# A norm's reciprocal taken of a quarter of its elements and carried to all partitions by a store and a load

## The reference

```python
def rms_norm(x, g):
    xf = x.astype(jnp.float32)
    y = xf * lax.rsqrt(jnp.mean(xf * xf, axis=-1, keepdims=True) + RMS_EPS)
    return (y * g.astype(jnp.float32)).astype(x.dtype)

def short_conv_mixer(h, w_in, conv_w, w_out):
    bcx = h @ w_in
    b_gate, c_gate, xp = bcx[..., :D], bcx[..., D:2 * D], bcx[..., 2 * D:]
    u = c_gate * xp
    u_conv = causal_depthwise_conv3(u, conv_w)
    return (b_gate * u_conv) @ w_out

def swiglu(h, w_gate, w_up, w_down):
    return (jax.nn.silu(h @ w_gate) * (h @ w_up)) @ w_down

for i in range(2):
    h = h + mixer_i(rms_norm(h, mixer_norm[i]))      # attention, then convolution
    h = h + swiglu(rms_norm(h, ffn_norm[i]), w_gate[i], w_up[i], w_down[i])
return rms_norm(h, final_norm)
```

## Time and profile before

| | |
|---|---|
| median of 3 runs | 1054.24 us (1054.06 to 1055.86) |
| the profiled execution's own time | 1052.55 us |
| its span, first to last instruction | 1050.6 us |
| TensorE busy | 1041.8 us (99%) |
| VectorE busy | 908.9 us (87%) |
| ScalarE busy | 556.6 us (53%) |
| mean granted TensorE clock | 0.999 of full speed |

### The profile page before, as it was taken

How to read it: one execution, slowest core, us unless ns; L and a number is a source line. 1 busy time by engine, 2 the same in 40 slices (tenths; PEclk the granted TensorE clock), 3 DMA queues, 4 the chain that set the end, 5 groups by cost and what they waited for, 6 DMA issues and landing times. The chain is left out here.

```text
span 1050.6 us, 18481 instructions
## 1 busy us (share of the span) xinstructions
PE 1041.8 (99%) x7018; PEld 959.4 (91%) x7018; DVE 908.9 (87%) x1291; ACT 556.6 (53%) x801; POOL 46.6 (4%) x28
## 2 busy tenths in 40 slices
PE   9999999999999999999999999999999999999998
PEld 7888888899999999889888999888999999988897
DVE  6787775999999998997879988699999999899685
ACT  6678883745554555633344434355555545563432
POOL 0342230000000000000000000000000000000000
PEclk9999999999999999999999999999999999999999
DMA  8121212233233233223222332322332232223212
GB/s 339 53 71 50 75 46 80 81 121 110 92 117 120 87 113 110 75 107 121 85 107 90 111 122 80 112 90 81 120 120 93 106 120 102 88 101 120 81 71 80
DMA packets 16972, 106.29 MB, mean 101 GB/s; under 512 B 1888, under 2 KB 2272, under 8 KB 6432
## 3 DMA queue, kind: packets, MB, share of 16 engines
q1 hardware_dynamic: 16416, 104.60, 27.7%
q10 hardware_dynamic: 432, 0.83, 0.2%
q0 software_dynamic: 80, 0.26, 0.1%
HBM read 103.59 MB, written 2.10 MB: 101 GB/s over the span
## 5 line engine op out<-in xcount | busy, mean ns | idle before, releaser
L511 PE MATMUL bank<-x_hi,split 128*128 128x256 f32 (+1 forms) x704 | 203.6, 289 | 0.1
L513 PE MATMUL bank<-x_hi,split 128*128 128x256 f32 (+1 forms) x704 | 203.4, 289 | 0.0
L512 PE MATMUL bank<-x_lo,split 128*128 128x256 f32 (+1 forms) x704 | 203.3, 289 | 0.0
L511 PEld LDWEIGHTS bank<-x_hi,split 128*128 128x128 f32 x704 | 132.3, 188 | 3.4 <-DVE split L1521 0.6
L511 PE MATMUL bank<-x_hi,s_hi 128*128 128x256 f32 x480 | 134.3, 280 | 0.4 <-ACT work L1238 0.4
L513 PEld LDWEIGHTS bank<-x_hi,split 128*128 128x128 f32 x704 | 132.3, 188 | 2.5
L512 PEld LDWEIGHTS bank<-x_lo,split 128*128 128x128 f32 x704 | 132.3, 188 | 2.5
L513 PE MATMUL bank<-x_hi,s_lo 128*128 128x256 f32 x480 | 133.9, 279 | 0.0
L512 PE MATMUL bank<-x_lo,s_hi 128*128 128x256 f32 x480 | 133.8, 279 | 0.0
L1903 DVE TENSOR_TENSOR split<-raw,split 128x2048 fp32r<-128x2048 f32 x54 | 123.6, 2289 | 11.7 <-ACT split L1228 10.6
L1228 ACT ACTIVATE split<-raw 128x2048 fp32r<-128x2048 f32 x54 | 103.4, 1916 | 46.2 <-PE bank L513 25.9
(11 more groups left out here) (289 smaller groups left out, 2469.9 us busy)
## 6 DMA issues: line engine op xcount, KB each, us to landing
raw<-weights_in SPq DMA_DIRECT2D x82, 1024.0 KB, 4.8
raw<-weights_in SPq DMA_DIRECT2D x12, 768.0 KB, 4.2
work<-x SPq DMA_DIRECT2D x4, 512.0 KB, 12.9
raw<-weights_in SPq DMA_DIRECT2D x4, 512.0 KB, 3.7
out<-head SPq DMA_DIRECT2D x3, 512.0 KB, 2.7
head<-head_in SPq DMA_DIRECT2D x1, 768.0 KB, 9.3
first_raw<-weights_in SPq DMA_DIRECT2D x3, 192.0 KB, 5.4
first_raw<-weights_in SPq DMA_DIRECT2D x1, 576.0 KB, 8.0
```

Of the source, the lines that this page charges most:

```text
L511: pe.matmul(o, lhs[0], rhs[0], start=start, stop=False, skip_group_check=True)
L512: pe.matmul(o, lhs[0], rhs[1], start=False, stop=False, skip_group_check=True)
L513: return pe.matmul(o, lhs[1], rhs[0], start=False, stop=stop, skip_group_check=True)
```

## The change

Three things change. First, the square root and the reciprocal. ScalarE takes the root in four pieces: partitions 32q to 32q+31 take the 128 tokens of quarter q, into a tile `rms_part` of 128x128; this also frees the bank. VectorE takes the reciprocal of that tile. SP stores it to a buffer in memory (64 KB), waits for the store, and loads rows 0, 32, 64 and 96 to all 128 partitions of `rstd` (256 KB, pieces of 512 bytes). Both DMAs stand on SP's queue among the weight loads, behind the two rounds of loads that open each FFN and the convolution. Second, VectorE works on `forms_split(0)` before it waits for the landing and scales the first gate chunk; in the convolution the reciprocal moves ahead of `forms_split(0)` and the wait stands behind it. Third, on ScalarE a Silu of one column stands ahead of the two real ones, and in the first product group `blocks_hi(1)` goes between the copies of product 1 and product 5, where both copies went first.

```diff
+        rms_part = sb("rms_part", P)
+        rms_rows = nc.dram_tensor("rms_rows", (P, P), F32).ap()
...
+            def spread_inverse():
+
+                n = T.add("inverse")
+                sp.wait_ge(rms_inverted, n)
+                sp.dma_start(rms_rows, rms_part[:, :]).then_inc(inverse_stored, 16)
+                sp.wait_ge(inverse_stored, 16 * n)
+                rows = rms_rows.rearrange("(q r) n -> q r n", q=TOK)[:, 0, :]
+                sp.dma_start(rstd[:, :].rearrange("p (q n) -> p q n", q=TOK), rows.partition_broadcast(P)).then_inc(rstd_landed, 16)
...
             for layer in range(2):
-                c = loads(c, KF // 2, [SLOT] * 2)
+                c = loads(c, 2, [SLOT] * 2)
+                spread_inverse()
+                c = loads(c, KF // 2 - 2, [SLOT] * 2)
...
                 if layer == 0:
-                    c = loads(c, 8, [SLOT] * 2)
+                    c = loads(c, 2, [SLOT] * 2)
+                    spread_inverse()
+                    c = loads(c, 6, [SLOT] * 2)
...
             def rms(b, width):
 
                 act.wait_ge(stat_summed, T.add("stat"))
-                act.activation(bank[b][:, :], bank[b][:, :], ACT.Sqrt, bias=eps[:, 0:1], scale=1.0 / width).then_inc(rms_done, 1)
+                for q in range(TOK):
+                    rows, cols = slice(q * P // TOK, (q + 1) * P // TOK), slice(q * P, (q + 1) * P)
+                    part = act.activation(rms_part[rows, :], bank[b][rows, cols], ACT.Sqrt, bias=eps[rows, 0:1], scale=1.0 / width)
+                part.then_inc(drained[b], 1)
...
                 sums_hi_of(0)
+                act.activation(silu_scratch[:, :], eps[:, :], ACT.Silu)
                 act.wait_ge(drained[1], T.add("b1"))
...
-                gate(copy_first=True)
+                copy(0, 1)
+                blocks_hi(1)
+                copy(0, 5)
+                sums_hi_of(1)
+                copy(0, 6)
+                copy_last(0, 0)
...
-            act.wait_ge(stat_summed, T.add("stat"))
-            act.activation(rstd[:, :], bank[6][:, :], ACT.Sqrt, bias=eps[:, 0:1], scale=1.0 / D).then_inc(drained[6], 1)
+            rms(6, D)
...
             def inverse_rms(b):
 
-                v.wait_ge(rms_done, T.add("rms"))
-                drain(b, v.reciprocal(rstd[:, :], bank[b][:, :]))
-                landed(b)
+                v.wait_ge(drained[b], T.add(f"b{b}"))
+                v.reciprocal(rms_part[:, :], rms_part[:, :]).then_inc(rms_inverted, 1)
+
+            def inverse_spread():
+
+                v.wait_ge(rstd_landed, 16 * T.add("inverse"))
...
                 inverse_rms(4)
+                forms_split(0)
+                inverse_spread()
                 scaled(3, 0)
                 scaled(4, 1)
-                forms_split(0)
                 forms(1)
...
             done(0)
+            inverse_rms(6)
             forms_split(0)
-            v.wait_ge(drained[6], T.add("b6"))
-            do(v.reciprocal(rstd[:, :], rstd[:, :]))
-            settle()
+            inverse_spread()
             do(v.tensor_tensor(rstd2, rstd[:, :], rstd[:, :], ALU.mult))
```

More of the change, by code:

```diff
@@ L231, in build @@
         eps, act_scratch = numbers[:, 9 * TOK:9 * TOK + 1], numbers[:, 9 * TOK + 1:9 * TOK + 2]
+        silu_scratch = numbers[:, 9 * TOK + 2:9 * TOK + 3]
         bank = [ctx.enter_context(nc.psum_tensor(f"bank{b}", [P, SEQ], F32)) for b in range(8)]
@@ L325, in build @@
         rms_done = sem("rms_done")
+        rms_inverted, inverse_stored, rstd_landed = sem("rms_inverted"), sem("inverse_stored"), sem("rstd_landed")
         silu_done = sem("silu_done")
```

## The result

The change makes the kernel slower: 1066.18 us in the median (six runs, 1064.59 to 1073.89) against 1054.08 before (six runs, 1052.61 to 1055.86). The ratio is 1.0127, with an interval of 1.0107 to 1.0147, so about 12 us are lost where I had forecast 1.7 won (1052.5 us, in a range from 1051.9 to 1056.0). The profiled execution after has a span of 1066.1 us and took 1067.9; the one of before, 1050.6 and 1052.55, was among the quickest of its kernel and this one is somewhat above its median, so the two traces lie 15.5 us apart and not 12.1.

The account below looks back on a forecast made before the run. TensorE was taken as the bound, busy 1041.8 of 1050.6 us. Gains of 0.73 (convolution), 0.49 (first FFN) and 0.45 (second FFN) made 1.7 us, from the median 1054.24 to 1052.5, range 1051.9 to 1056.0.

Parts of the forecast that it names:

- 256 KB broadcast, 3.3 us: Load of the reciprocals to all partitions at each norm, priced between weight loads at 3.3 us.
- the end that I had given it, 6.8: Upper end for the broadcast's time: 6.8 us, from the trace's only broadcast, issued by POOL during the crowded start.
- x: Time from the small reciprocal's end to the broadcast's landing: handoffs, store and broadcast, 6.0 us, ends 4.6 and 11.1.
- the two handoffs: SP's delay from a result to its issue, before store and before broadcast: 0.2 us each, 0.4 in all.
- the far end: Longest trip considered, 11.1 us with both transfers at their worst: a loss of 4.9 + 4.7 + 3.5, or 13 us.
- I expect no other transfer beside it: Assumption in pricing the broadcast at 3.3 us: nothing else would be transferring while it was under way.
- The points from which each place loses: Trip lengths where gain ends: second FFN 5.6 us, first FFN 6.2, convolution 7.6; FFNs then lose 1 us per us.
- the prediction's three terms: Losses in first FFN, second FFN and convolution once the trip is too long; 4.9, 4.7 and 3.5 us at 11.1.
- the pause at 751: TensorE's old loss in the second FFN, 0.95 us, of which some 0.85 was to go.
- the whole rival 0.12: Slower: a longer wait for the landing, losing over 2.1 us from a trip of 7.45; 1058.0 at 8; chance 0.12.
- the first stall at the copy of product 5: Second FFN: TensorE would wait 0.4 us near 732 for this ScalarE copy, now behind blocks_hi(1).
- The prize: All TensorE loses behind the three norms, 0.49 + 0.73 + 0.95, 2.2 us: the most a short trip could return.

Follow-up runs that it names:

- e4: The change, but SP waits for the broadcast to land before issuing the next weight load: 1061.27 us, ratio 1.0075 to the kernel before.
- e1: The change, but only rows 0, 32, 64, 96 are stored, side by side, and loaded as one 2 KB row per partition: 1050.46 us, ratio 0.9973.
- e2: The change, but four loads of 32 partitions, each partition reading its own row of each quarter: 1050.54 us, ratio 0.9972.
- e6: The change, but only the four rows are stored, 1 KB apart instead of 16 KB, still read by all partitions: 1050.61 us, ratio 0.9958.
- e7: The change, but the load's 512 pieces each come from their own address in the weights (output not the norm's): 1050.66 us, ratio 0.9957.
- e11: The change, but only the four rows are stored, 16.5 KB apart, still read by all partitions: 1050.33 us, ratio 0.9979.
- e12: The one-row version e1 with the store made and waited for twice, for a longer trip: 1056.32 us, ratio 1.0035.
- e10: The change, but only the four rows are stored, 4 KB apart, still read by all partitions: 1058.69 us, ratio 1.0063.
- e3: The change's reordering alone: one root and the full 128x512 reciprocal at the new place, no store or load: 1053.25 us, ratio 0.9994.
- e9: The change, but only the four rows are stored, kept 16 KB apart, still read by all partitions: 1068.06 us, ratio 1.0145.
- e5: The change, but its load is cut in four, all partitions still reading rows 0, 32, 64, 96: 1065.05 us, ratio 1.0102.

## Why the prediction was wrong

- **The step that failed is the term "256 KB broadcast, 3.3 us" of the round trip.** It measured 9.0 in the median, above even the end that I had given it, 6.8. The others of x held or were kinder: the two handoffs of 0.4 in all are 0.03 and some 0.02 in the timelines, the store 1.5 where I took 2.3. x was to be 6.0 and was 11.4, 10.6 and 10.5; the far end had been 11.1.
- **What stands in its place.** Of the excess of 5.7 us, 4.0 are the addresses (7.3 in e4, where nothing is beside it, and 3.3 in e1), and 1.7 the load of weights beside it (9.0 less 7.3). "I expect no other transfer beside it" was against a line of my own: I had worked out that the load leaves at about 219.2, and it left at 219.32, while the broadcast would have been on its way until 221.9 by my own sum. I asked only whether the weights had cover, and not what they do to the transfer ahead of them.
- **The bounds of the piece size.** I priced the broadcast between weight loads, whose rows are eight and more times as long (512 KB on 128 partitions is 4 KB each), and allowed for "small pieces" in a word. The size proved harmless (e2, e6, e7, e11: 512 bytes each, 1.8 to 3.6 us). The property that mattered, four source rows 16 KB apart read by all 128 partitions, stood in the diff and had no row at all in the trace. There the upper end of 6.8 was no real bound.
- **The mechanism was right.** Landing, scalings, forms, `blocks_hi(1)`, copy of product 5: 4.95 us from the start of the forms to the end of that copy (228.39 to 233.34), against 5.0. The points from which each place loses held too. What each costs TensorE, matmul by matmul, beside what the prediction gives for the measured x:

  | place, loses from | e12: x, cost | e4: x, cost | the change: x, cost | by the prediction |
  |---|---|---|---|---|
  | first FFN, 6.2 | 7.4, 1.1 | 9.0, 2.7 | 11.4, 6.5 (1.4 of it the clock) | 1.2, 2.8, 5.2 |
  | second FFN, 5.6 | 7.3, 1.5 | 8.9, 3.1 | 10.5, 4.7 | 1.7, 3.3, 4.9 |
  | convolution, 7.6 | 6.5, -0.8 | 8.9, 1.6 | 10.6, 3.3 | -0.7, 1.3, 3.0 |

  At the x of the change the prediction's three terms and the pause at 751 that goes make 12.1 us in all; the places measured 13.5 with the clock's share, on which the prediction has no word, and 12.1 without it. That these two agree to 0.1 us is partly luck: the convolution cost 0.3 more than priced, the FFNs 0.1 or 0.2 less. The far end of the prediction, 13 us at x = 11.1 with both transfers at their worst, has the size of the result, but only the broadcast was at its worst and beyond, the store was not, and I had given the whole rival 0.12.
- **One step of it missed.** I had the first stall at the copy of product 5. At so long a trip it comes one copy earlier, as the Silus stand ahead of the copy of product 1 on ScalarE: 2.96 us there, 0.35 at product 5. The sum stays, the place changes.
- **What the four roots and the small Silu cost.** The reciprocal took 0.95, as said. The roots took 1.48 us, near the upper end of 0.66 to 1.56, and made the reciprocal of the convolution wait 0.29. In the FFNs they lie in ScalarE's idle time, and nothing came of the early table load.
- **The prize was right.** Of 2.2 us for a short trip, e1 got 1.9 against the quickest run of before in its batch (1052.38 less 1050.46) and e11 2.1 from median to median (1052.48 less 1050.33). Matmul by matmul e1 has won 2.5 at the three places; the 0.3 more lie in the second FFN before 745 us, where I had found no pause. The ratios of e6 and e7 show more, and in their batch the kernel before ran mostly in the slowest of the three clusters of times told of below.

**A version that beats both kernels** is e11, or e1: 0.9979 (0.997 to 0.9988) and 0.9973 (0.9962 to 0.9984) of the kernel before, 16 us under the change. Either differs from the change in the buffer's shape and the rows that are stored.

## What to carry to other kernels

Where a few rows that all partitions read lie in memory can price their broadcast more than its bytes do: the same 256 KB took 3.2 us or 9.1. Keep the rows in one piece, or try another distance (1 KB and 16.5 KB were good where 4 KB and 16 KB were bad), and where the trace has no transfer of the same address pattern, treat the nearest row as no bound. When a transfer enters a queue, ask what is issued behind it while it is on its way, and not only whether that has cover. And before work is taken off an engine, count what the engine behind it waits for: 7.2 us of VectorE were worth some 2.2 at best, and for this prize a trip was put on the path that loses a microsecond for each that it is late.

## What the runs showed of the hardware that was not expected

- 512 reads of 512 bytes, all of the same four rows, land in 3.2 to 3.6 us when the rows are 1 or 16.5 KB apart, 6.7 at 4 KB and 9.1 at 16 KB, all with a load of weights behind them. While the slow broadcast is under way, the DMA engines are a quarter busy and move little, though the load of weights was issued at 219.32; only when the broadcast is nearly through do the weights arrive. SP's windows, after (length, granted clock, DMA share, GB/s):
```profile
219.00:220.00 1.00, 1.00 0.25 45
...
222.00:223.00 1.00, 1.00 0.25 35
...
225.00:226.00 1.00, 1.00 0.84 324
```
- The matmuls of the FFN loops run at one of two paces at a granted clock of 1.00. The first line is of the profile before, the second of that after, the same window:
```profile
300.00:350.00 50.00, 50.00 (x431) 1.00 0.32 114
```
```profile
300.00:350.00 50.00, 50.00 (x427) 1.00 0.29 105
```
 That is 1%, and 1.6 us for an FFN. The times of the kernel before lie in three clusters near 1052.4, 1054.1 and 1055.8, as if none, one or both FFNs ran slower. The profiles of e1, e2, e6, e7 and e11 show 431 in both FFNs, and all their times lie within 1.1 us; e10 and the profile before show 431 in both too, e12 and e3 have 427 in both, and in the others one of the two FFNs is slow. All the kernels that have no pause of TensorE behind the norms show the quick pace, but that the pauses set it is not shown, and what picks the level stays open.
- After the change TensorE's granted clock was at its lower level, 1.2 GHz, behind an idle time of 2.96 us in the first FFN and of 2.76 in the second, and at 2.4 GHz behind one of 2.69 in the convolution. e9 has it low behind 2.79 in the convolution (0.54 from 577 to 580 us) and high behind 2.57 and 2.85 in its FFNs; e5 has it low behind 2.51 in the convolution (0.59 from 576 to 578 us) and high behind 2.60 in the second FFN. So the length of that one idle time does not tell which it will be.
